# A weight chunk loaded into a free buffer beside the ring, a split moved ahead of another, and a split given to GpSimd

## The reference

```
x += NSA(rmsnorm(x));       x += ConvGLU(rmsnorm(x))          # layer 0
k, v = rmsnorm_kv(x) @ kv_w                                    # shared keys and values
x += DiffAttn(rmsnorm(x), k, v);  x += ConvGLU(rmsnorm(x))     # layer 1
out = rmsnorm(x)
```

```
o = rmsnorm(o, subln_g) * (1.0 - lam_init)      # per head of 128 columns, 8 heads
x = x + o.reshape(B, S, 1024) @ w_out           # diff_w_out, 1024 x 1024
h = rmsnorm(x, ffn_norm_g)
u = h @ w_in                                    # 1024 x 5504
# causal convolution of 3 taps over the tokens, gate and value halves
x = x + (silu(gate) * val) @ ffn_w_out          # 2752 x 1024
```

## Time and profile before

| | us |
|---|---|
| median of 3 runs | 645.58 (645.19 to 645.89) |
| the profiled execution | 645.72 |
| its span, first to last instruction | 643.9 |
| TensorE busy | 627.6 (97%) |
| VectorE busy | 523.9 (81%) |
| ScalarE busy | 420.9 (65%) |
| GpSimd busy | 32.4 (5%) |
| TensorE's mean granted clock | 0.991 |

### The profile page before, as it was taken

One profiled execution on the slowest core, in us unless ns is written; L12 is line 12 of the kernel. 1 busy time (PEld: TensorE's weight loads), 2 busy tenths in 40 slices (PEclk: granted clock), 3 DMA queues, 4 the chain that ended last, 5 costly groups with the idle time before them and its releaser, 6 DMA issues.

```text
span 643.9 us, 10674 instructions
## 1 busy us (share of the span) xinstructions
PE 627.6 (97%) x3596; PEld 525.5 (82%) x3596; DVE 523.9 (81%) x947; ACT 420.9 (65%) x824; POOL 32.4 (5%) x70
## 2 busy tenths in 40 slices
PE   9999999999999999999999999997999999999995
PEld 8988666679888888888888877785988888888894
DVE  6687688757998888889988677465899888888887
ACT  6755477748666666666668666755766666666666
POOL 0000023300000000000012000310000000000000
PEclk9999999999999999999999999998999999999998
DMA  8967130035565555555527646203455555555521
GB/s 329 346 227 273 42 155 3 1 135 178 200 219 191 184 184 183 189 178 191 196 79 269 231 162 238 99 1 131 163 196 198 196 196 196 191 181 188 188 70 66
DMA packets 21744, 110.16 MB, mean 171 GB/s; under 512 B 2640, under 2 KB 3024, under 8 KB 12752
## 3 DMA queue, kind: packets, MB, share of 16 engines
q1 hardware_dynamic: 21424, 109.53, 47.3%
q10 hardware_dynamic: 288, 0.22, 0.1%
HBM read 108.68 MB, written 1.05 MB: 170 GB/s over the span
## 4 chain that ended last, share of the span: by engine, by line
PE 87%; DVE 8%; ACT 3%; issue 1%; DMA 1%; DVEq 0%; ACTq 0%
PE psU L713 21%; PE psA L502 13%; PE psA L503 13%; PE psA L504 13%; PE psU L718 10%; PE psU L929 2%; PE psA L889 1%; DVE win_lo L1818 1%; PE psU L914 1%; PE psU L1089 1%; DVE arena L1937 1%; DVE arena L2230 1%; PE psU L693 1%; DMA stage<-in_w_ffn_in 1%; PE psU L692 1%
## 5 line engine op out<-in xcount | busy, mean ns | idle before, releaser
L713 PE MATMUL psU<-hA,win_hi 128*128 128x512 f32 x608 | 190.8, 395 | 0.0
L718 PEld LDWEIGHTS psU<-hA,win_lo 128*128 128x128 f32 x608 | 114.2, 188 | 26.6
L718 PE MATMUL psU<-hA,win_lo 128*128 128x256 f32 x608 | 119.4, 278 | 0.0
L1911 DVE TENSOR_TENSOR win_lo<-stage,win_hi 128x1024 fp32r<-128x1024 f32 x86 | 104.8, 1221 | 0.0
L713 PEld LDWEIGHTS psU<-hA,win_hi 128*128 128x128 f32 x608 | 95.2, 189 | 2.8
L1383 ACT ACTIVATE win_hi<-stage 128x1024 fp32r<-128x1024 f32 x89 | 93.3, 1050 | 3.5 <-PE psA L504 3.5
L1937 DVE SCALAR_TENSOR_TENSOR arena<-arena,prm 128x255 f32<-128x255 f32 (+1 forms) x168 | 77.2, 480 | 3.7 <-ACT arena L1395 0.7
L502 PE MATMUL psA<-wout_hi,act_hi 128*128 128x512 f32 x168 | 65.9, 392 | 0.3
L503 PE MATMUL psA<-wout_lo,act_hi 128*128 128x512 f32 x168 | 65.5, 390 | 0.0
L504 PE MATMUL psA<-wout_hi,act_lo 128*128 128x512 f32 x168 | 65.4, 389 | 0.0
L1395 ACT ACTIVATE arena<-arena,prm 128x256 f32<-128x256 f32 x84 | 46.0, 595 | 26.1 <-DVE arena L1958 21.2
(11 more groups left out here) (316 smaller groups left out, 1130.4 us busy)
## 6 DMA issues: line engine op xcount, KB each, us to landing
stage<-in_w_ffn_in SPq DMA_DIRECT2D x44, 1024.0 KB, 4.8
stage_out<-in_w_ffn_out SPq DMA_DIRECT2D x44, 516.0 KB, 5.0
stage<-in_w_kv SPq DMA_DIRECT2D x8, 1024.0 KB, 4.8
stage<-in_w_dq SPq DMA_DIRECT2D x4, 1024.0 KB, 4.9
stage<-in_w_group SPq DMA_DIRECT2D x3, 1024.0 KB, 4.8
stage<-in_w_nsa_out SPq DMA_DIRECT2D x3, 1024.0 KB, 4.9
stage<-in_w_phi SPq DMA_DIRECT2D x2, 1024.0 KB, 5.9
stage<-in_w_dout SPq DMA_DIRECT2D x2, 1024.0 KB, 5.2
```

The source lines that it names most:

```text
L713: mm(o, win_hi[:, slot, cs], hA[:, k, :, :].rearrange("p a q -> p (a q)"), start=k == 0, stop=False)
L718: last = mm(o[:, 0:S], win_lo[:, slot, cs], hA_hi[:, k2, :], start=False, stop=k2 == KT - 1)
L1911: last = dve.tensor_tensor(win_lo[:, win, cs], stage[:, slot, cs], win_hi[:, win, cs].bitcast(F32), sub)
```

## The change

Three edits, all at the way from layer 1's attention to its FFN.

1. The first chunk of the second FFN (C_F1) is no longer loaded into `stage`, but into phi_k1 (now also called ffn_first), where C_DO + 1 lay. SyncE issues it when C_DO + 1 is fully split (in_lo and the new half_split, the renamed kv_half, which VectorE's first half of C_DO + 1 now adds to as well) and when ScalarE has made the high parts of C_DO + 2. It signals on the same semaphore as before. ScalarE and VectorE read the chunk from there (`first_of`).
2. In layer 1 the split of the last output chunk, split(first - 1), and heads_hi(3) / heads_lo(3) come ahead of the FFN's first splits, on both engines. In layer 0 the order stays.
3. GpSimd makes the low parts of C_DO + 2, the whole chunk in one instruction of 2048 columns, once ScalarE's high parts are there. VectorE's split of it goes; VectorE waits for in_lo to count it ahead of split(first - 1).

```diff
+                    if layer and j == 0:
+                        sp.wait_ge(sem["in_lo"], C_DO + 2)
+                        sp.wait_ge(sem["half_split"], 2)
+                        sp.wait_ge(sem["in_hi"], 2 * (C_DO + 3))
+                        sp.dma_start(ffn_first[:, :], a_ffn_in[layer, 0]).then_inc(stage_full[first % 2], 16)
+                        continue
                     load_main(first + j, a_ffn_in[layer, j], W)
...
+            pool.wait_ge(sem["in_hi"], 2 * C_DO + 6)
+            pool.tensor_tensor(win_lo[:, win_of(C_DO + 2), :], stage[:, stage_of(C_DO + 2) % 2, :],
+                               win_hi[:, win_of(C_DO + 2), :].bitcast(F32), ALU.subtract).then_inc(sem["in_lo"], 1)
...
@@ scalar, first_splits
                     split_out(0, 0, layer > 0)
                     split_in(0, 0, 0)
-                    split(first - 1)
+                    if layer == 0:
+                        split(first - 1)
@@ scalar, ffn
                     heads_hi(2)
+                    split(first - 1)
+                    heads_hi(3)
                     first_splits()
-                    heads_hi(3)
@@ vector, ffn
                 if layer:
                     heads_lo(2)
+                    dve.wait_ge(sem["in_lo"], first - 1)
+                    split(first - 1)
+                    heads_lo(3)
                 split_out(0, 0)
                 split_in(0, 0, 0)
-                split(first - 1)
-                if layer:
-                    heads_lo(3)
+                if layer == 0:
+                    split(first - 1)
@@ vector, ahead of ffn(1, ...)
             scale_heads(dve, 3, "sub1_scaled")
-            dve.wait_ge(sem["in_lo"], C_DO + 2)
-            split(C_DO + 2)
```

More of the change, by code:

```diff
@@ L138 @@
 in_hi in_lo in_used out_hi last_hi out_lo out_used conv_params
-newton norm_step xT_bank xT_hi xT_lo square mean_sq eps_ready mean0 root rstd rstd_t row_src row_bank row_ready half_lo y_ready last_lo kv_half w0_hi w0_half
+newton norm_step xT_bank xT_hi xT_lo square mean_sq eps_ready mean0 root rstd rstd_t row_src row_bank row_ready half_lo y_ready last_lo half_split w0_hi w0_half
 proj_act proj_dve rope_t1 rope_t2 rope_done gate_z gate_e gate_e1 gates_ready
@@ L213, in build @@
         d_out1 = phi_k1
+        ffn_first = phi_k1
         d_squares = qT[:, :, :].rearrange("p k q -> p (k q)")
@@ L350, in side_of, with first_of @@
             return {C_FREE: vals_flat, C_EARLY: keysT, C_WO: keysT, C_DO: d_out0, C_SIDE: d_out1}[s]
+        def first_of(layer, slot):
+            return ffn_first if layer else stage[:, slot, :]
         def pv_out(u):
@@ L523, in project @@
                         if half == 1:
-                            pe_.wait_ge(sem["kv_half"], 1)
+                            pe_.wait_ge(sem["half_split"], 1)
                     elif s0 + half > 1:
@@ L1371, in split_in @@
                         act.wait_ge(stage_full[slot], 16 * loads_of(stage_of(first)))
-                        act.activation(wout_hi[:, 1, :], stage[:, slot, 0:W // 2], ACT.Copy).then_inc(sem["w0_hi"], 1)
+                        act.activation(wout_hi[:, 1, :], first_of(layer, slot)[:, 0:W // 2], ACT.Copy).then_inc(sem["w0_hi"], 1)
                         return
@@ L1382, in split_in @@
                         act.wait_ge(sem["in_used"], first + 1)
-                    act.activation(win_hi[:, win_of(first + b), h * W // 2:(h + 1) * W // 2], stage[:, slot, h * W // 2:(h + 1) * W // 2],
+                    src = first_of(layer, slot) if isinstance(j, int) and j == 0 else stage[:, slot, :]
+                    act.activation(win_hi[:, win_of(first + b), h * W // 2:(h + 1) * W // 2], src[:, h * W // 2:(h + 1) * W // 2],
                                    ACT.Copy).then_inc(sem["in_hi"], 2 if isinstance(j, int) and j == 0 else 1)
@@ L1820, in split @@
                         last.then_inc(sem["in_lo"], 1)
-                    elif s == C_KV + 1:
-                        last.then_inc(sem["kv_half"], 1)
+                    elif s in (C_KV + 1, C_DO + 1):
+                        last.then_inc(sem["half_split"], 1)
             def split_piece(s, i):
@@ L1906, in split_in @@
                         dve.wait_ge(sem["w0_hi"], layer + 1)
-                        dve.tensor_tensor(wout_lo[:, 1, :], stage[:, slot, cs], wout_hi[:, 1, :].bitcast(F32), sub).then_inc(sem["w0_half"], 1)
+                        dve.tensor_tensor(wout_lo[:, 1, :], first_of(layer, slot)[:, cs], wout_hi[:, 1, :].bitcast(F32), sub).then_inc(sem["w0_half"], 1)
                         return
@@ L1910, in split_in @@
                     win = win_of(first + b)
-                    last = dve.tensor_tensor(win_lo[:, win, cs], stage[:, slot, cs], win_hi[:, win, cs].bitcast(F32), sub)
+                    src = first_of(layer, slot) if isinstance(j, int) and j == 0 else stage[:, slot, :]
+                    last = dve.tensor_tensor(win_lo[:, win, cs], src[:, cs], win_hi[:, win, cs].bitcast(F32), sub)
                     if h == 1:
```

## The result

The changed kernel takes 640.93 us, the kernel before 645.74 in the same runs: ratio 0.9923, 95% interval 0.9910 to 0.9937. That is 4.8 us less; 5.3 were forecast (640.2), and the time lies in the stated range. (One of its six runs took 3539 us and stands outside the comparison.) The profiled execution took 640.93 us, its span is 639.1.

A forecast was written before the change was run, and what follows sets the result against it. TensorE, busy 627.6 of 643.9 us, was taken as the bound, with only its pauses and clock to win: 6.93 us gained less 1.6 lost to GpSimd's hold, 645.58 - 5.33 = 640.2 us, range 638.4 to 643.0.

The forecast's parts named there:

- The three terms that go: On TensorE: 0.38 us wait at L629, 4.05 us pause at the last chunk, 2.50 us of lowered clock; sum 6.93.
- 0.4 us of slack at the adds to x: Ahead of the raw transposes: first add to x ends at 5.4, TensorE wants it at 5.93; the second has as much.
- the slack at the last output chunk: Last input ready 1.9 us after the transposes at 438.94, TensorE needs it after 3.18: 1.3 us of slack.
- the 2.50 us for the clock: Twelve matmuls after the pause take 5.25 us at the lowered clock, about 2.75 at the full: 2.50 us saved.
- The loss by the hold: GpSimd's 2048-column instruction holds VectorE's root operation L324 until 432.24; TensorE's transposes come at 435.5, not 433.9: 1.6 us lost.
- the handover from VectorE to TensorE: Between VectorE's first scaling and TensorE's transposes of it: 0.15 us, which left 0.66 us of slack.
- Rival A: GpSimd's instruction holds nobody, so the full 6.93 us is gained: 638.7 us; chance 0.17.
- C: Slower than before, GpSimd's operation being much longer than twice its half: at 9 us, 647 us; chance 0.06.
- B: The hold is there and TensorE's new 1.4 us pause lowers the clock, costing 2.5 us: 642.7 us; chance 0.17.
- The sum: Whole kernel: 6.93 us gained less 1.6 lost to the hold gives 5.33 less, 640.2 us; chance 0.56.
- 0.3 us of scatter: Allowance on each side of the range from A to B, giving 638.4 to 643.0 us.

The follow-up runs named there:

- repeat: The changed kernel run again with no edit: 640.36 us, ratio 0.9919 to the kernel before.
- order alone: Against the changed kernel: FFN chunk loaded into the ring as before, VectorE splits C_DO + 2, only the new order kept; 639.34 us, ratio 0.9903 to before.
- load alone: Against the changed kernel: old order on both engines, VectorE splits C_DO + 2, only the moved load kept; 639.58 us, ratio 0.9903 to before.
- GpSimd's part alone: Against the changed kernel: ring load and old order, only GpSimd's 2048 columns kept; 640.74 us, ratio 0.9916 to before.
- GpSimd later: The changed kernel with 832 more columns for GpSimd ahead of its instruction, result unread; 643.86 us, ratio 0.9965 to before.

## Why the prediction held, and where it was off

**The three terms that go: right.** From the heads' transposes (L1191, before 433.90; after L1203, 436.07) to the raw transposes it is 17.52 us before and 10.53 after: 6.99 less, where the sum said 6.93. Granted clock 1.00 from 436 to 452 after, 0.79 before. The 0.4 us of slack at the adds to x sufficed: TensorE waits nowhere there. Two sizes inside it were off: the slack at the last output chunk was 1.07 us and not 1.3, as ScalarE started heads_hi(3) 0.63 behind the transposes instead of 0.45 (441.33 against 440.70). And the 2.50 us for the clock are those of one execution of before: in the 17 runs of it that go with the last experiments, the six with a mean granted clock of 0.995 took 644.8 to 645.4 us, the eight with 0.991 took 646.1 to 648.2. That suggests that what the fallen clock costs differs from execution to execution; the prediction took it as fixed.

**The loss by the hold: right in mechanism, 0.24 too large.** From the split of C_DO + 1 to the heads' transposes it is 15.01 us before and 16.37 after: 1.36 lost, 1.6 forecast. GpSimd took 4.62, not 4.74. And I gave the handover from VectorE to TensorE 0.15; after, the first scaling ends at 436.01 (435.32 + 0.69) and TensorE starts at 436.07, so there was 0.75 of slack, not 0.66. In all, VectorE's second step of the root began 2.11 late (432.91 against 429.99, each from the stretch's start), where I had put 2.25. Rival A (nothing held) and C (GpSimd far longer) fall by this row, and B by the windows: a pause of 1.2 us did not lower the clock, in the one profile of this kernel and in its repeat, and the other comparable runs of both list a mean granted clock of 0.996 to 0.998 as well.

**The sum: 5.3 forecast, 5.6 in the stretch, 4.8 in the medians.** The terms, as measured, account for 5.63 of the profile; what hides 0.8 of it lies ahead of the stretch, which began anywhere in a span of 1.2 us in the ten profiles here. I had allowed 0.3 us of scatter. The repeat's median, with a stretch that began only 0.09 later than before's in its profile, differs from before by 5.4. So two deviations of opposite sign stand in the first profile, and how near its median came to 640.2 is in part chance: the hold cost 0.24 less than forecast, the late start added 0.8.

**What the prediction did not say.** It described the load as what makes the gain possible. The runs show it is one of three sufficient ways: order alone, load alone and GpSimd's part alone each remove the pause. I had the rows for the order at least (the load needs 4.80 us from 436.00, and by my own count ScalarE asks for it after 440; it did at 440.89), and asked only what the three do together. They are not equally safe: the order leaves 1.1 us of slack, the load alone and GpSimd's part alone 0.2. The largest finding is thus that the edit which costs, GpSimd's long instruction, isn't needed beside the others. Half of it, short enough to end as VectorE's root begins, even gains 0.5 us over leaving all of it to VectorE.

## What to carry to other kernels

When several edits aim at one wait, work out each alone: here any one of the three took the whole gain, and the others must be judged by their price and by the slack they add. Before giving work to GpSimd, list what VectorE does while the instruction runs: here a chain of tiny steps on operands in SBUF waited for the end of the 4.6 us instruction, while the two reads from PSUM passed, and a piece that ended as the chain began cost nothing. And a pause of TensorE may cost more than its length, by the clock behind it: 3.9 us of it cost 6.5 in the profile of before.

## What was not expected of the hardware

- A VectorE operation with a single operand in SBUF can be held too: L289, a scaling of 8 int32 columns, took 1.23 us beside GpSimd's last piece and 0.17 otherwise. L326, of the same kind, began 0.01 us ahead of the third piece and took 0.16; that piece then took 1.29. At 99.01 such an operation was only 0.17 longer beside GpSimd, so that row is weaker support for a hold to the end than the prediction took it for.
- The clock can fall after TensorE is back at work: in "GpSimd later" matmuls started at 438.18 at the full clock, and 0.50 was granted from about 438.4 to 441.8. Before, it stayed at 0.50 for 6.74 us.
- A pause of 3.1 us lowered the clock in some executions of one kernel only: eight of twelve, by their mean granted clock of 0.991 to 0.995. One of 1.1 to 1.2 us lowered it in none of the profiles here.
- The same start of the kernel is not equally long in each execution: the stretch began at 418.62 to 419.86 us in ten profiles, with 26 warm-up matmuls of 4.60 to 5.92 us. Where the difference arises beyond these matmuls is not shown.
